# Modulation vector by 24 multiply-and-sum instructions of VectorE instead of TensorE products

## The reference

```python
def conv_ffn(h, w_up, w_conv, b_conv, w_down):
    u = h @ w_up
    u = depthwise_conv_of_width_3(u, w_conv) + b_conv
    val, gate = jnp.split(u, 2, axis=-1)
    return (jax.nn.silu(gate) * val) @ w_down

def second_block(x, c, ada_w, ada_b, norm_g, w_in, ...):
    mod = jnp.einsum('bd,de->be', jax.nn.silu(c), ada_w[0]) + ada_b[0]      # 1024 x 3072 weight
    shift, scale, gate = jnp.split(mod, 3, axis=-1)
    h = _rmsnorm(x, norm_g[0]) * (1.0 + scale[:, None, :]) + shift[:, None, :]
    p = jnp.einsum('bsd,de->bse', h, w_in[0])
    ...
    x = x + gate[:, None, :] * out
    return _rmsnorm(x, final_g)
```

## Time and profile before

| | us |
|---|---|
| runs before, median of 3 (lowest, highest) | 1135.39 (1134.3, 1137.38) |
| the profiled execution's own time | 1135.28 |
| its span, first to last instruction | 1133.5 |
| busy: PE, DVE, ACT | 1074.1, 809.3, 637.7 |
| busy: PE in `ada` (line 652, x96) | 15.3 |
| mean granted TensorE clock | 0.994 of full |

### The profile page before, as it was taken

One profiled execution on the slowest core, in us unless ns is written; L12 is line 12 of the kernel. 1 busy time (PEld: TensorE's weight loads), 2 busy tenths in 40 slices (PEclk: granted clock), 3 DMA queues, 4 the chain that ended last, 5 costly groups with the idle time before them and its releaser, 6 DMA issues.

```text
span 1133.5 us, 25869 instructions
## 1 busy us (share of the span) xinstructions
PE 1074.1 (95%) x10950; PEld 1006.2 (89%) x10950; DVE 809.3 (71%) x1329; ACT 637.7 (56%) x898; POOL 6.5 (1%) x15
## 2 busy tenths in 40 slices
PE   4999999999999998899999988999999999999997
PEld 3999889898989887899999978889889888889997
DVE  4964577757666775787677675789889889955573
ACT  5844565535444664655455556656658567667343
POOL 0000000000000000000000000000000000000000
PEclk9999999999999999999999989999999999999999
DMA  7552266676844441436555734333323232224531
GB/s 244 155 181 90 70 209 232 223 273 213 285 154 149 157 140 38 146 133 205 185 185 173 234 108 152 113 113 113 113 81 124 99 105 85 76 76 133 196 119 38
DMA packets 132991, 167.69 MB, mean 148 GB/s; under 512 B 2657, under 2 KB 124513, under 8 KB 131489
## 3 DMA queue, kind: packets, MB, share of 16 engines
q1 hardware_dynamic: 131632, 153.51, 41.6%
q0 software_dynamic: 1264, 12.78, 2.8%
HBM read 164.18 MB, written 2.10 MB: 147 GB/s over the span
## 4 chain that ended last, share of the span: by engine, by line
PE 79%; DVE 12%; ACT 6%; issue 2%; DMA 1%; SPq 0%; DVEq 0%; ACTq 0%
PE bank L310 16%; PE bank L311 14%; PE bank L312 14%; DVE wl L272 2%; PE banks L616 2%; PE bank L620 2%; PE bank L618 2%; PE bank L616 2%; PE banks L620 2%; PE banks L618 2%; ACT wh L267 2%; DVE hf L2364 2%; PE bank L652 1%; PE banks L1126 1%; PE bank L1158 1%
## 5 line engine op out<-in xcount | busy, mean ns | idle before, releaser
L310 PE MATMUL bank<-xh,wh 128*128 128x256 f32 x1360 | 397.7, 292 | 0.6 <-DVE wl L272 0.6
L311 PE MATMUL bank<-xl,wh 128*128 128x256 f32 x1392 | 393.5, 283 | 0.0
L312 PE MATMUL bank<-xh,wl 128*128 128x256 f32 x1360 | 384.3, 283 | 0.0
L272 DVE TENSOR_TENSOR wl<-raw,wh 128x2048 fp32r<-128x2048 f32 x97 | 221.4, 2286 | 83.4 <-ACT wh L267 83.3
L310 PEld LDWEIGHTS bank<-xh,wh 128*128 128x128 f32 x1360 | 259.9, 191 | 9.8 <-issue 2.8
L311 PEld LDWEIGHTS bank<-xl,wh 128*128 128x128 f32 x1392 | 266.5, 191 | 0.8 <-issue 0.7
L312 PEld LDWEIGHTS bank<-xh,wl 128*128 128x128 f32 x1360 | 260.2, 191 | 0.0
L267 ACT ACTIVATE wh<-raw 128x2048 fp32r<-128x2048 f32 x97 | 184.6, 1906 | 48.7 <-PE bank L620 38.8
L296 DVE TENSOR_TENSOR wl<-raw,wh 128x1024 fp32r<-128x1024 f32 x86 | 103.7, 1217 | 22.9 <-ACT wh L288 22.7
L2364 DVE SCALAR_TENSOR_TENSOR hf<-big,vecs,hf 128x256 f32<-128x256 f32 x240 | 101.4, 478 | 0.0
L288 ACT ACTIVATE wh<-raw 128x1024 fp32r<-128x1024 f32 x86 | 87.6, 1057 | 8.8 <-PE bank L312 5.5
(11 more groups left out here) (393 smaller groups left out, 2234.4 us busy)
## 6 DMA issues: line engine op xcount, KB each, us to landing
raw<-in_ffn_w_up SPq DMA_DIRECT2D x44, 1024.0 KB, 5.1
raw<-in_w_in SPq DMA_DIRECT2D x36, 1024.0 KB, 5.5
raw<-in_ffn_w_down SPq DMA_DIRECT2D x22, 1024.0 KB, 5.0
raw<-in_gla_w_in SPq DMA_DIRECT2D x12, 1024.0 KB, 6.1
big<-in_ada_w POOLq DMA_DIRECT2D x8, 1536.0 KB, 8.3
raw<-in_attn_w_qkv SPq DMA_DIRECT2D x6, 1024.0 KB, 5.0
raw<-in_gla_w_out SPq DMA_DIRECT2D x4, 1024.0 KB, 5.1
raw<-in_attn_w_out SPq DMA_DIRECT2D x4, 1024.0 KB, 5.1
```

Of the source, the lines that this page charges most:

```text
L272: eng.tensor_tensor(WL[:, n % RING, :, :], RAW[:, n % RING, :, :], WH[:, n % RING, :, :].bitcast(F32), ALU.subtract).then_inc(w_lo_ready, 1)
L310: nc.tensor.matmul(ps, wh, xh, start=start, stop=False)
L311: nc.tensor.matmul(ps, wh, xl, start=False, stop=False)
L312: return nc.tensor.matmul(ps, wl, xh, start=False, stop=stop)
```

## The change

The weight comes transposed from the host (3072 x 1024, `ada_w_t`), so that 128 outputs lie on 128 partitions and the sum runs along the free dimension. The row `c` is spread by one DMA over all partitions (128 x 1024, into the gate tiles, which are free until the second block), and ACT applies the SiLU to it before the loop of layer 0. POOL loads 24 pieces of 128 x 1024 (0.5 MB) into three buffers. DVE handles each in one `scalar_tensor_tensor` that multiplies piece and row and gives out the sum (`accum_out`): 12 in each gated layer, one after HID in turns 0 to 8, and one more after the last `wl` split of turns 2, 4 and 6. DVE's loop is written out for this, PE's loop of layer 0 becomes a loop. `ada`, `mod_turned`, ACT's two copies, and their waits go. For layer 1, a preload of the SiLU's table stands ahead of ACT's loop.

```diff
@@ -488,10 +488,9 @@
 
-        ada_ring = [flat(40 + 12 * h, 12) for h in range(2)]
-        ada_rows = [flat(40 + 2 * h, 2) for h in range(2)]
-        sc_col = small[:, 0:8]
-        ada_v = a["ada_w_2"].rearrange("(k p) n -> p k n", p=P)
+        ada_ring = [flat(at, 4) for at in (16, 20, 40)]
+        SILU_C = GT.rearrange("p a m t -> p (a m t)")
+        MODS, MODS_FIRST = 24, 12
 
         @block.gpsimd
         def _(pool):
@@ -500,13 +499,16 @@
             pool.wait_ge(sem("u_zeroed"), 1)
             pool.dma_start(w_up[0:16, 0, :], a["gla_w_gate_up_f"]).then_inc(sem("rank_landed"), 16)
             pool.dma_start(w_up[16:32, 1, :], a["gla_w_gate_up_b"]).then_inc(sem("rank_landed"), 16)
+            pool.dma_start(SILU_C, a["c_row"].broadcast_to([P, D])).then_inc(sem("c_landed"), 16)
             pool.wait_ge(sem("rms_split"), 4)
             pool.wait_ge(sem("gla_out_split"), GH_)
             pool.wait_ge(sem("rstd_ready"), 2)
-            for k in range(KT):
-                if k >= 2:
-                    pool.wait_ge(sem("ada_summed"), k - 1)
-                pool.dma_start(ada_ring[k % 2], ada_v[:, k, :]).then_inc(sem(f"ada_landed{k % 2}"), 16)
+            for j in range(MODS):
+                if j >= 3:
+                    pool.wait_ge(sem("ada_summed"), j - 2)
+                if j == MODS_FIRST:
+                    pool.wait_ge(sem("attn_split"), QH)
+                pool.dma_start(ada_ring[j % 3], a["ada_w_t"][j * P:(j + 1) * P, :]).then_inc(sem(f"ada_landed{j % 3}"), 16)
 
@@ -628,30 +630,10 @@
                 product(pe, n0 + 1, 1, *EARLY[2 * layer + 1])
                 up(n0 + 2, 1, ready=ready)
                 down(n0 + 4, 0, first=True)
-                if layer == 0:
-                    for i in range(1, FI - 1):
-                        up(n0 + 2, 1, i)
-                        if i <= KT:
-                            ada(i - 1)
-                        down(n0 + 4, 0, i)
-                else:
-                    with pe.Fori(1, FI - 1) as i:
-                        up(n0 + 2, 1, i)
-                        down(n0 + 4, 0, i)
+                with pe.Fori(1, FI - 1) as i:
+                    up(n0 + 2, 1, i)
+                    down(n0 + 4, 0, i)
                 down(n0 + 3 * FI - 1, FI - 1, last=True)
-
-            def ada(k):
-
-                pe.wait_ge(sem(f"ada_landed{k % 2}"), 16 * (k // 2 + 1))
-                if k == 0:
-                    pe.wait_ge(sem("silu_c_ready"), 1)
-                    pe.wait_ge(sem("rstd_ready"), 2)
-                scaled = sc_col[:, k:k + 1].broadcast_to([P, 32])
-                for j in range(6):
-                    q = 32 * (j % 4)
-                    last = nc.tensor.matmul(PS[2 + j // 4][q:q + 32, :], scaled, ada_ring[k % 2][:, j * 512:(j + 1) * 512],
-                                            start=k == 0, stop=k == KT - 1, skip_group_check=True)
-                last.then_inc(sem("ada_summed"), 1)
 
             def start_product(n):
 
@@ -885,15 +866,6 @@
                                                 skip_group_check=True)
                 if pair == 3:
                     last.then_inc(block_done, 1)
-
-            def mod_turned():
-                for h in range(2):
-                    rows = P - 64 * h
-                    for q in range(4):
-                        last = nc.tensor.matmul(PS[3][:, 16 * h + q:16 + 8 * h:4],
-                                                ada_rows[h][0:rows, q * P:(q + 1) * P], ident[0:rows, 0:rows:32],
-                                                start=True, stop=True)
-                last.then_inc(sem("mod_summed"), 1)
 
             def half_of(j, m):
 
@@ -1402,6 +1373,11 @@
                                          ACT.Copy).then_inc(evacuated, 1)
 
                 split_hi(act, n0 + 3)
+                if layer == 0:
+                    act.wait_ge(sem("c_landed"), 16)
+                    nc.scalar.activation(SILU_C, SILU_C, ACT.Silu).then_inc(sem("silu_c_ready"), 1)
+                else:
+                    nc.scalar.preload_act_table(ACT.Silu)
                 act.wait_ge(evacuated, (E_F1 if layer else E_F0) + 2)
                 with act.Fori(0, FI - 1) as i:
                     hidden_hi(layer, 0, i)
@@ -1552,9 +1526,6 @@
             mlp(0, N_F0)
 
-            act.wait_ge(sem("ada_summed"), KT)
-            nc.scalar.activation(ada_rows[0], PS[2][:, :], ACT.Copy).then_inc(sem("ada_rows_ready"), 1)
-            nc.scalar.activation(ada_rows[1][0:64, :], PS[3][0:64, :], ACT.Copy).then_inc(sem("ada_rows_ready"), 1)
             early(2, lambda k: ("norm_mix", 8 + k))
             split_hi(act, N_QKV + 2)
             norm_split(2)
@@ -1969,12 +1940,30 @@
                             else:
                                 ch.done(ins)
 
-                def hidden(s, i=0):
-                    dve.wait_ge(sem("gate_silu"), g1 + s + 1 + i)
-                    if s or not isinstance(i, int):
-                        dve.wait_ge(sem("val_convolved"), g0 + s + 1 + i)
+                def modulation(j):
+
+                    dve.wait_ge(sem(f"ada_landed{j % 3}"), 16 * (j // 3 + 1))
+                    if j == 0:
+                        dve.wait_ge(sem("silu_c_ready"), 1)
+                    v.scalar_tensor_tensor(ada_ring[j % 3], ada_ring[j % 3], 1.0, SILU_C, ALU.mult, ALU.mult,
+                                           accum_out=mod[:, j:j + 1]).then_inc(sem("ada_summed"), 1)
+
+                def modulation_whole():
+                    dve.wait_ge(sem("ada_summed"), MODS)
+                    ch.step(v.tensor_tensor(mod[:, 0:24], mod[:, 0:24], vec("ada_b_2", 0, 24), ALU.add))
+                    ch.done(v.scalar_tensor_tensor(mod[:, 24:32], mod[:, 8:16], 1.0, vec("norm_g_2", 0, KT),
+                                                   ALU.add, ALU.mult))
+
+                def hidden(i):
+                    dve.wait_ge(sem("gate_silu"), g1 + i + 1)
+                    if i:
+                        dve.wait_ge(sem("val_convolved"), g0 + i + 1)
                     v.tensor_tensor(HID, SGT, CV, ALU.mult).then_inc(sem("hidden_ready"), 1)
-                    dve.wait_ge(sem("hidden_hi"), g1 + s + 1 + i)
+                    if i < 9:
+                        modulation(MODS_FIRST * layer + i + sum(u < i for u in (2, 4, 6)))
+                    elif layer:
+                        modulation_whole()
+                    dve.wait_ge(sem("hidden_hi"), g1 + i + 1)
                     v.tensor_tensor(GL[:, 0:2, :], HID, GH[:, 0:2, :].bitcast(F32), ALU.subtract)\
                         .then_inc(sem("hidden_split"), 1)
 
@@ -1985,21 +1974,21 @@
                 times_rstd(U[:, 1, :, 1:T + 1], 1)
                 dve.wait_ge(evacuated, e0 + 2)
                 convolve(CG, 1, 0, ch)
-                def round_of(i, s=1):
-                    split_lo(dve, n0 + RING * s + 1, i)
-                    hidden(s - 1, i)
-                    dve.wait_ge(evacuated, e0 + 1 + 2 * s + 2 * i)
-                    convolve(CV, 0, s, ch, i)
-                    split_lo(dve, n0 + RING * s + 2, i)
-                    dve.wait_ge(evacuated, e0 + 2 + 2 * s + 2 * i)
-                    convolve(CG, 1, s, ch, i)
-
-                with dve.Fori(0, FI - 2) as i:
-                    ch.enter(i, 10)
+                def round_of(i):
+                    split_lo(dve, n0 + 4, i)
+                    hidden(i)
+                    dve.wait_ge(evacuated, e0 + 3 + 2 * i)
+                    convolve(CV, 0, 1, ch, i)
+                    split_lo(dve, n0 + 5, i)
+                    dve.wait_ge(evacuated, e0 + 4 + 2 * i)
+                    convolve(CG, 1, 1, ch, i)
+
+                for i in range(FI - 1):
                     round_of(i)
-                    split_lo(dve, n0 + 6, i)
-                ch.leave(FI - 2)
-                round_of(0, FI - 1)
+                    if i < FI - 2:
+                        split_lo(dve, n0 + 6, i)
+                        if i in (2, 4, 6):
+                            modulation(MODS_FIRST * layer + i + i // 2)
                 for m in range(2):
                     dve.wait_ge(sem("gate_silu"), g1 + FI + m)
                     if m == 0:
@@ -2286,10 +2275,6 @@
             out_lo(QH - 2)
             out_lo(QH - 1)
 
-            dve.wait_ge(sem("mod_summed"), 1)
-            ch.step(v.tensor_tensor(mod[:, 0:24], PS[3][:, 0:24], vec("ada_b_2", 0, 24), ALU.add))
-            ch.step(v.scalar_tensor_tensor(mod[:, 24:32], mod[:, 8:16], 1.0, vec("norm_g_2", 0, KT), ALU.add, ALU.mult))
-
             second_ffn = lambda k: ("norm_ffn", 8 + k)
             add_projection(N_AOUT, 4, X, (3, second_ffn), lo_from=1)
 
@@ -2585,6 +2570,8 @@
     }
     for n in _WEIGHTS:
         arrays["in_" + n] = np.ascontiguousarray(np.asarray(inputs[n])[0])
+    arrays["in_ada_w_t"] = np.ascontiguousarray(np.asarray(inputs["ada_w_2"])[0].T)
+    arrays["in_c_row"] = np.ascontiguousarray(np.asarray(inputs["c_2"]).reshape(1, D))
     for n in ("ffn_w_up", "ffn_w_down"):
```

(12 more changed lines are left out.)

## The result

The changed kernel takes 1123.74 us, the median of four runs (1122.51 to 1124.17). The kernel before, run between them, takes 1136.39 us (1134.3 to 1138.6). The ratio is 0.9888, with a 95% interval of 0.9871 to 0.9905: faster by 12.65 us. The forecast was 1120.7 us and -14.66 us; the measured time lies in its range, in the upper half.

The account below looks back on a forecast made before the run. PE was taken to bound the kernel, with 79% of the chain and no idle time in the turns. -16.16 - 0.68 + 0.82 + 1.36 = -14.66 us from 1135.39 gave 1120.7 us, range 1117.8 to 1125.7.

Parts of the forecast that it names:

- Part 1: First gated layer's turns on PE: the 96 `ada` instructions go, 8 groups of 2.02 us, -16.16 us.
- Part 2: End of attention: `mod_turned` goes and `out_part` starts earlier, after a wait for DVE's write, -0.68 us.
- after such a write PE starts about 0.15 us later: End of attention: delay from DVE's low-half write to PE's `out_part`, taken from `gl` writes, about 0.15 us.
- Part 3: 24 DVE multiply-and-sums at 1.22 us each: free in later turns, +0.82 us in the two layers' first turns.
- the 0.09 us for the read of the accumulator: DVE's modulations: handing out the sum adds 0.09 us to 1.13 us, giving 1.22 us each.
- Rival A: DVE's modulations: the sum halves the rate, 2.3 us each, first turns pay 2.1 us more, 1122.8 us; 20%.
- Part 4: Start: the 0.5 MB spread row goes ahead of the last piece of `consts`, delaying PE, +1.36 us.
- Rival C: Start: the spread row is hidden and `consts` lands as before, 1119.3 us; 10%.
- The edits costed at nothing: ACT's SiLU and table load, its removed copies and in-turn table load, DVE's moved small steps: no cost or gain.
- TensorE's clock is no term of this sum: First turns of both layers: half-pace products, 1.5 us lost in the first, counted only in the range.
- the base: Whole kernel before the change: 1135.39 us, median of three runs, profiled execution 1135.28 us, from which the gain was subtracted.
- Rival B: First turns: PE's clock lower in both layers, 1122.2 us, or in neither, 1119.2 us; 15%.

Follow-up runs that it names:

- experiment 4: The changed kernel with a second multiply-and-sum of the same size on DVE behind each of the 24, its result unused: 1126.73 us.
- experiment 2: The kernel before, plus the 0.5 MB DMA of the row at the start, its data unused: 1138.94 us, ratio 1.0011 to before.
- experiment 1: The changed kernel with the DMA that spreads the row issued at about 135 us instead of 3.6 us: 1120.58 us.
- experiment 7: The changed kernel without its 24 multiply-and-sum instructions, so the modulation is not computed; transfers and the rest stay: 1122.02 us.
- experiment 6: Both kernels again, unchanged, for further profiles: before 1138.32 and 1137.71 us in two executions, the changed kernel 1122.01 us.
- 5: The changed kernel with the row fetched at about 135 us and turn 0's modulation moved behind that turn's last wl split: 1120.53 us, ratio 0.9862 to before.

## Why the prediction came out as it did

**Part 1, -16.16 us: right.** The turns went from 19.30 to 17.28 us, and the turns hold that length with twice the work on DVE too (experiment 4).

**Part 2, -0.68 us: right, the size off by 0.1.** Taken at equal waits it is 140.70 - 139.93 = 0.77 us. The step "after such a write PE starts about 0.15 us later" was read from another write; here it is 0.06 us. That a wait takes the place of the removed work, and leaves less than half of its 1.86 us as gain, held.

**Part 3, +0.82 us: the mechanism right, the size 0.66.** The waits grew by 0.30 and 0.36 us. The mis-sized term is the 0.09 us for the read of the accumulator, taken from ACT's row. On DVE the read takes 78 to 86 ns in its record and nothing of the engine's time:

```profile
L1948 DVE SCALAR_TENSOR_TENSOR big<-big,gate_tiles x24: 1212/1218/1222, 187.1 to 619.7; 128x1024 f32<-128x1024 f32 x24
L1948 DVE DVE_READ_ACCUMULATOR big<-big,gate_tiles x24: 78/83/86, 188.3 to 620.8; 128x1 f32 x24
```

**Rival A is refuted by the same rows**: 1218 ns with the sum, 1222 without it. The rule of the Trainium skill (*Vector Engine (DVE) Microarchitecture Reference*, section 7) that this form with two fp32 sources in SBUF runs at half throughput does not hold for this instruction; the measurement decides.

**Part 4, +1.36 us: right for the row.** The profiles give 1.2 to 1.7, the timed runs 1.3 (experiment 2), 3.2 (experiment 1 against the change's first runs) and 1.4 (against its second). Rival C falls: `consts` does not land as before. Not in the sum are the some 0.7 us by which the changed program starts later without the row as well.

**The edits costed at nothing** cost nothing that shows: the turns keep their 17.28 us with no modulation (experiment 7), with one and with two (experiment 4).

**The steps that failed: "TensorE's clock is no term of this sum", and the base.** Rival B had the price (1.5 us for a layer) and the condition (the longer waits of part 3), but was given 15% and left out of the sum. In the second layer it came in all four profiles with the longer wait. And the sum was made against one execution, whose start, as experiment 6 shows, was of the cheaper kind: 5.21 us of sums and no piece at half pace near 36 us, where two other executions of before pay 1.3 and 1.5 us more, as the change's first profile did. Of the 3.2 us between the forecast 1120.7 and the profiled 1123.89, the start holds 4.6 - 1.36 = +3.2, the second layer's first turn +1.5, parts 2 and 3 together -0.3, the program behind the second layer, where the change lost less at the lower clock, -1.5, and what lies outside the span +0.35.

So two terms of 1.5 us that the sum lacks, one in the second layer and one behind it, cancel, and that the sum comes out as near as it does is in part luck. The start is of one kind or the other by the moment in either kernel. By the medians over all runs, 1122.9 for eight of the change and 1137.3 for thirty of before, the gain is 14.5 us, close to the sum's 14.66, and the forecast time is too low by about as much as its base was, 2 us.

## What to carry to other kernels

Work taken off the bounding engine counts in full where that engine has no idle time; work added to another engine in its idle gaps is free here, except at the one place where the bounding engine waits for it, and that place should be looked for first: here the first turn of each loop. A wait of TensorE can cost more than its length, since products behind it may run at 1.2 GHz for a while, so a term that lengthens a wait is to be given the price of that too. And where a kernel's times fall in two groups 3 us apart, one profile is no base for a forecast to a microsecond: see which group it is of.

## What the runs showed of the hardware

A `scalar_tensor_tensor` of VectorE over 128x1024 fp32 takes 1218 ns with a sum along its row, as long as without (1222), and its accumulator read of 83 ns lies beside the next instruction.

A transfer of 0.5 MB that reads one row 128 times, issued by another queue at the same moment as the 1 MB that PE waits for, made that land later: PE's first product came 1.7 us later with it in the kernel before, 1.2 in the changed one.

After a gap of 2.23 us TensorE was granted 1.2 GHz for about 3 us of the second layer's first turn, three times in three, and after 1.88 us not once in seven; after 3.38 us for longer. In the first layer's first turn no length of the wait told this apart: after 1.93 to 1.95 us it came in five profiles of seven, and after 3.40 us it lasted no longer than after 2.23. At the same place of the start, near 36 us, one and the same kernel got 1.2 GHz in some executions and 2.4 in others (a granted clock of 0.83 and 1.00 over the same 10 us), which cost 1.5 us; in three further kernels, 4, 5 and 7, it cost 3 us there.
